# Modulation weights loaded two tiles at a time in a two-block transformer kernel on one Trainium2 core

## What is computed

```python
def _layer(x, ...):                       # first block, two layers
    proj = _rms_norm(x, g_pre) @ w_in     # 2048 -> 5952 columns
    ...                                   # three kinds of attention, gated
    y = concat([o_a, o_b, o_c]) @ w_out   # 2048 -> 2048
    return x + _rms_norm(y, g_post)

def hybrid_layer(x, c, ..., w_mod, b_mod, ...):   # second block, two layers
    mod = silu(c) @ w_mod + b_mod                 # (1, 2048) @ (2048, 6144)
    shift, scale, gate = split(mod, 3)
    h = rms_norm(x, g_pre) * (1.0 + scale) + shift
    ...                                           # window attention, spatial gating, linear attention
    out = y @ w_out
    return x + gate * rms_norm(out, g_post)
```

## Time and profile before

| what | value |
|---|---|
| runs | 3788.1, 3803.92 and 3804.02 us, median 3803.92 |
| profiled execution, own time | 3796.71 us |
| its span, first to last instruction | 3795.0 us |
| mean granted TensorE clock | 0.964 of full |
| PE busy | 3564.3 us, 94% |
| DVE busy | 1820.6 us, 48% |
| ACT busy | 1111.3 us, 29% |
| POOL busy | 221.5 us, 6% |
| DMA | 430.32 MB, mean 113 GB/s |

### The profile page before, as it was taken

The page is one execution under the profiler, slowest core; times in us unless marked ns, Lnnn a source line. Parts: engine busy times, 40 slices in busy tenths (PEclk is TensorE's granted clock), DMA queues, the critical chain, the costliest instruction groups (busy, mean ns, idle before and its releaser), DMA issues.

```text
span 3795.0 us, 51974 instructions
## 1 busy us (share of the span) xinstructions
PE 3564.3 (94%) x17037; PEld 2820.2 (74%) x17037; DVE 1820.6 (48%) x3194; ACT 1111.3 (29%) x1784; POOL 221.5 (6%) x410
## 2 busy tenths in 40 slices
PE   6999999899799999988997999999997999999998
PEld 5777877658677787775786888788786888778786
DVE  4554664434555547643356332635544432625553
ACT  3232242122222322510323222532322322522331
POOL 1101001001211010010010000000000000000000
PEclk9999999989999999998998999999898999999999
DMA  7625415115655353150354333032143333033142
GB/s 231 192 94 185 138 34 168 57 35 190 207 179 185 103 189 92 41 174 12 112 176 151 98 96 98 18 97 78 56 150 108 89 100 99 23 92 100 45 144 99
DMA packets 186920, 430.32 MB, mean 113 GB/s; under 512 B 21238, under 2 KB 28849, under 8 KB 180312
## 3 DMA queue, kind: packets, MB, share of 16 engines
q1 hardware_dynamic: 151720, 302.30, 24.6%
q0 software_dynamic: 32064, 104.44, 9.4%
q10 hardware_dynamic: 2928, 21.02, 1.3%
HBM read 406.61 MB, written 24.75 MB: 114 GB/s over the span
## 4 chain that ended last, share of the span: by engine, by line
PE 77%; DMA 10%; DVE 7%; issue 5%; ACT 1%; DVEq 0%; POOLq 0%; SPq 0%; ACTq 0%; POOL 0%
PE bank L635 19%; PE bank L637 19%; PE bank L636 19%; DMA wmod<-in_w_mod 9%; PE bank L676 4%; PE bank L694 3%; PE bank L668 2%; PE bank L685 2%; DVE macc L1327 2%; PE bank L827 1%; PE bank L655 1%; PE bank L805 1%; PE bank L816 1%; PE bank L664 1%; PE bank L881 1%
## 5 line engine op out<-in xcount | busy, mean ns | idle before, releaser
L635 PE MATMUL bank<-wlo,act_hi 128*128 128x512 f32 (+1 forms) x3968 | 1558.1, 393 | 49.8 <-DVE zone L1356 28.5
L637 PE MATMUL bank<-whi,act_lo 128*128 128x512 f32 (+1 forms) x3968 | 1541.0, 388 | 0.0
L636 PE MATMUL bank<-whi,act_hi 128*128 128x512 f32 (+1 forms) x3968 | 1541.0, 388 | 0.0
L1014 ACT ACTIVATE whi<-stage 128x1024 fp32r<-128x1024 f32 (+1 forms) x496 | 515.1, 1048 | 1512.6 <-PE bank L637 644.8
L635 PEld LDWEIGHTS bank<-wlo,act_hi 128*128 128x128 f32 x3968 | 749.5, 189 | 228.9 <-DVE zone L1356 33.1
L1312 DVE TENSOR_TENSOR wlo<-stage,whi 128x1024 fp32r<-128x1024 f32 (+1 forms) x496 | 597.0, 1208 | 624.4 <-ACT whi L1014 620.6
L637 PEld LDWEIGHTS bank<-whi,act_lo 128*128 128x128 f32 x3968 | 749.1, 189 | 153.4
L636 PEld LDWEIGHTS bank<-whi,act_hi 128*128 128x128 f32 x3968 | 749.9, 189 | 146.5
L1327 DVE SCALAR_TENSOR_TENSOR macc<-wmod,csil,macc 128x512 f32<-128x512 f32 x360 | 270.4, 751 | 440.0 <-DMA wmod<-in_w_mod 432.7
L2053 POOL DMA_DIRECT2D wmod<-in_w_mod x384 | 206.2, 537 | 1793.7 <-DVE macc L1322 1054.5
L1120 ACT ACTIVATE zone<-bank 128x512 f32<-128x512 f32 x128 | 76.4, 597 | 149.2 <-PE bank L685 149.0
(11 more groups left out here) (211 smaller groups left out, 2508.0 us busy)
## 6 DMA issues: line engine op xcount, KB each, us to landing
stage<-in_w_in SPq DMA_DIRECT2D x352, 512.0 KB, 3.7
wmod<-in_w_mod POOLq DMA_DIRECT2D x384, 256.0 KB, 3.2
stage<-in_w_out SPq DMA_DIRECT2D x128, 512.0 KB, 3.9
out<-Y ACTq DMA_DIRECT2D x20, 1024.0 KB, 5.1
zone<-out SPq DMA_DIRECT2D x4, 4096.0 KB, 14.5
stage<-in_w_in SPq DMA_DIRECT2D x16, 320.0 KB, 4.2
Y<-in_x SPq DMA_DIRECT2D x4, 1024.0 KB, 9.2
rpb_tiles<-rpb_pad POOLq DMA_DIRECT2D x16, 224.0 KB, 7.2
```

The source lines that it names most:

```text
L635: pe.matmul(out, hi_x, lo_w, start=(k == 0), stop=False)
L636: pe.matmul(out, hi_x, hi_w, start=False, stop=False)
L637: mm = pe.matmul(out, lo_x, hi_w, start=False, stop=(k == KC - 1))
L1014: act.activation(whi[:, j % RH, :, 0:width], stage[:, j % RS, :, 0:width], ACT.Copy)\
```

## The change

`wmod` becomes two places of two tiles each, 8 KB in a partition. `mprod` and `junk` lose memory of their own and lie over the second pair, so the total and all addresses behind them stay. A load takes two tiles (512 KB) in one DMA and waits until the pair before the last is used; the credit is 4. VectorE waits once for each pair. In the first block ScalarE writes the squares to `zone` at column `ZK`; in the second, to `mprod` and `junk` as before. What is loaded, summed and multiplied, and in which order VectorE does it, stays.

```diff
-        wmod = sb("wmod", [P, 2, PW])
-        mprod = sb("mprod", [P, PW])
-        junk = sb("junk", [P, PW])
+        wmod = sb("wmod", [P, 2, 2, PW])
...
+        mprod = sb("mprod", [P, PW], at=wmod_at + 8 * PW)
+        junk = sb("junk", [P, PW], at=wmod_at + 12 * PW)
...
-        mod_landed = [count(f"mod_landed{s}", 16 * NIN * KC // 2, 0) for s in range(2)]
-        mod_used = count("mod_used", NIN * KC, 0, credit=2)
+        mod_landed = [count(f"mod_landed{s}", 16 * NIN * KC // 4, 0) for s in range(2)]
+        mod_used = count("mod_used", NIN * KC, 0, credit=4)
...
-                    act.activation((mprod, junk)[t % 2][:, :], LIN[t][:, :], ACT.Square,
+                    squares = (mprod, junk)[t % 2][:, :] if blk else view(ZK + t % 2 * PW, PW)
+                    act.activation(squares, LIN[t][:, :], ACT.Square,
...
             def mod_pair(l, q, i):
+                dve.wait_ge(mod_landed[i % 2].sem, mod_landed[i % 2].at(0, l, 16 * (q * (KC // 4) + i // 2 + 1)))
                 for k in (2 * i, 2 * i + 1):
                     m = q * KC + k
-                    dve.wait_ge(mod_landed[k % 2].sem, mod_landed[k % 2].at(0, l, 16 * (q * (KC // 2) + i + 1)))
                     if k == 0:
                         dve.wait_ge(mod_sum.sem, mod_sum.at(0, l, q))
                         apart(dve)
-                        dve.tensor_scalar(macc[:, :], wmod[:, 0, :], csil[:, 0:1], None, ALU.mult)\
+                        dve.tensor_scalar(macc[:, :], wmod[:, 0, 0, :], csil[:, 0:1], None, ALU.mult)\
...
-                        dve.scalar_tensor_tensor(out=macc[:, :], in0=wmod[:, k % 2, :], scalar=csil[:, k:k + 1],
+                        dve.scalar_tensor_tensor(out=macc[:, :], in0=wmod[:, i % 2, k % 2, :], scalar=csil[:, k:k + 1],
...
             def mod_loads(l, p):
-                for k in range(KC):
-                    pool.wait_ge(mod_used.sem, mod_used.at(0, l, p * KC + k + 1 - 2))
+                for i in range(KC // 2):
+                    pool.wait_ge(mod_used.sem, mod_used.at(0, l, p * KC + 2 * i + 2 - 4))
                     apart(pool)
-                    src = io["w_mod_2"][bass.ds(l, 1), k * P:(k + 1) * P, bass.ds(p * PW, PW)]
-                    pool.dma_start(wmod[:, k % 2, :], src.rearrange("o p n -> (o p) n"))\
-                        .then_inc(mod_landed[k % 2].sem, 16)
+                    src = io["w_mod_2"][bass.ds(l, 1), 2 * i * P:(2 * i + 2) * P, bass.ds(p * PW, PW)]
+                    pool.dma_start(wmod[:, i % 2, :, :], src.rearrange("o (a p) n -> p (o a) n", p=P))\
+                        .then_inc(mod_landed[i % 2].sem, 16)
```

More of the change, by code:

```diff
@@ L200, in build @@
         cgw = sb("cgw", [P, KC, G_RANK], at=wmod_at + 2432)
-        cgw_hl = sb("cgw_hl", [P, KC, 2, G_RANK], F32R, at=sb_at["mprod"])
-        la = sb("la", [P, TT, 256], at=sb_at["junk"])
-        assert sb_at["macc"] == sb_at["junk"] + 4 * PW
+        cgw_hl = sb("cgw_hl", [P, KC, 2, G_RANK], F32R, at=wmod_at + 8 * PW)
+        la = sb("la", [P, TT, 256], at=wmod_at + 12 * PW)
+        assert sb_at["macc"] == wmod_at + 16 * PW
         PP, ZQ, ZT, ZK, ZV = 0, 4096, 8192, 10240, 12288
```

## The result

The changed kernel takes 3748.67 us (median of four runs, 3748.2 to 3749.45) against 3801.41 us for the kernel before: a ratio of 0.9869, 95% interval 0.9846 to 0.9892, or 52.7 us less. The forecast was 3743 us, in a range of 3726 to 3784. The profiled execution's own time is 3749.45 us, its span 3747.8.

The account below looks back on a forecast made before the run. TensorE was taken as the bound, with late modulation tiles lengthening its panels. From the profiled execution's 3796.7 us, 57.3 came off and 0 was added for the start, 3739.4; half the distance to the median made 3743 us, range 3726 to 3784.

Parts of the forecast that it names:

- What bounds and what a wait costs: TensorE bounds; VectorE's 432.7 us wait for tiles counts only where TensorE stalls, through bank copies at panel ends.
- Distance, not number: Modulation loads: a reload issued a whole pair earlier hides its landing; fewer, larger loads are not what helps.
- L: Modulation loads: time from the end of a pair's use to the landing of its reload.
- budget of 9.4: Wide panels: us between a place's uses, two TensorE steps less one pair of accumulations; 4 us to spare.
- The sum: Panels 2, 10 and 11 return 49.4 us, six more panels 6.3, eleven others 1.6: 57.3 us in total.
- budget of 5.5 us: Narrow panels: two steps of 3.52 us less 1.5; a pair may come slightly late, costed at nothing.
- the bound of 5 us: Narrow panels: if the ring's cover is gone, 0.3 us in each of 16 steps.
- The start: Start of the kernel: the first two loads carry 1 MB rather than 512 KB; cost 0, at most 2.6 us.
- one common line: Start of the kernel: were all DMA traffic served in one line, the extra 0.52 MB would cost 1.3 to 2.6 us.
- A: Panels 10, 11 and 2: staged weights hold VectorE, about half of 49.4 us stays; 3772 us, chance 0.14.
- B: All 192 steps with modulation tiles: a pair's reload becomes the bound, 96 us lost; 3839 us, chance 0.04.
- C: Modulation loads: only one pair in flight, or the row sum's wait holds VectorE; no change, 3800 us, chance 0.06.

Follow-up runs that it names:

- the kernel before with copies first: Kernel before, loads unchanged; in eight panels with modulation tiles VectorE copies its two banks before the last pair of tiles: 3772.18 us, ratio 0.9942.
- the four places: Changed kernel with four places of one tile, one tile a load (384 loads of 256 KB): 3737.92 us, ratio 0.9851; run again, 3731.88 us.
- the single place: Changed kernel with 512 KB pair loads but one place and credit 2, each load waiting for the pair just used: 4107.39 us, ratio 1.081.
- the narrow panel's copies first: Changed kernel; in panel 10 alone VectorE copies its two banks before the last pair of tiles: 3736.72 us, ratio 0.9837; run again, 3733.91 us.
- squares alone: Kernel before with only the first block's squares written to `zone`: 3800.21 us over ten runs, ratio 0.9997.
- the run without reloads: Changed kernel with only the first four modulation tiles loaded and used over and over: 3739.84 us, ratio 0.9855.
- the runs with four and eight DMAs: Changed kernel with each pair loaded by four DMAs of 128 columns, 3763.89 us (0.9912), or eight of 64, 3895.87 us (1.0261).

## Why the prediction was right

**What bounds and what a wait costs.** Right. The 362 us of waiting that VectorE lost (432.7 less 71.1) brought 53 us, and they came where the price was read, in the length of panels. The reading that VectorE's bank copies behind a late pair carry it is shown by the kernel before with copies first, half the gain with the waits left in.

**Distance, not number.** Right, by the four places and the single place. The landing of a pair was taken as 4 to 5 us from the row for 512 KB on SP's queue; it is 4.5. L is 5.3 us against a budget of 9.4, so 4 us are to spare, as forecast. The Trainium skill (DMA: Bandwidth & Descriptors, section "Anatomy of one DMA — SWDGE (gpsimd) path") has 2.0 us plus the bytes at 436 GB/s, from which an estimate of 3.2 us follows; the measured landing is 1.3 us longer.

**The sum.** Panel 2 gave 12.4 of 12.5 us forecast, panel 10 18.2 of 18.7, panel 11 13.3 of 18.2. The whole was forecast as 57.3 us and is 55.7, read at the start of the second block. The three panels make 43.9 of it; the other panels and the starts of attention make 11.8, where 7.9 were in the sum. Of the surplus 1.5 us is TensorE's wait for Y at the start of attention, now 11.3 us and before 12.8, which the forecast had named and left out. The sum also left out three panels: it took eleven at 0.15 us, and beside panels 2 and 10 and the six of the earlier trace rows fourteen more take tiles, which would have made it 0.4 us larger. That the total is only 1.6 us off is partly luck: panel 11 was put 4.9 us too high and the other panels 3.9 too low.

**The step that was off.** "There a pair may come late by part of a microsecond. I cost that at nothing, since the ring of split weights lets VectorE run up to three steps ahead." The budget of 5.5 us was right and L is 5.3 to 5.8, so pairs are late by 0.4 us a turn; and the ring does cover the splits, for panel 10 itself is at 29.4. What it doesn't cover are the bank copies at the panel's end, which have no buffer ahead of them and stand behind the last pair. They cost 2 x 2.4 = 4.8 us. That this lies just under the bound of 5 us is luck: the bound was worked out for splits 0.3 us late in each of 16 steps, and the loss came by another way, as the narrow panel's copies first show.

**Smaller sizes.** VectorE's wait for tiles was to be below 40 us and is 71.1, all of the excess without effect but for panel 11. An issue takes POOL 0.711 us instead of 0.536, where up to twice as much had been allowed for. The start: the staged tile that matters lands 0.3 us later than in the earlier trace rows:

```profile
6.43 26.45 DMA stage<-in_w_in
```

The forecast was 0 with 2.6 as the bound. In two more profiles with the old loads (squares alone, and the kernel before with copies first) that tile landed at 32.75 and 33.29 us, before at 32.60 and after at 32.88, so the 0.3 lies inside the spread, and the larger load on POOL's queue doesn't hold up SP's by the 1.3 to 2.6 us of one common line. The rule cited from the Trainium skill (same page, section "Queues, rings and completion order"), turns between the queues that have work, agrees with this. It isn't free for every form: with the same bytes cut into 16 loads (eight DMAs a pair) the tile landed at 34.79, 1.9 us later than after the change. Squares: 0 forecast, none seen (ratio 0.9997).

**The predicted time.** It added half the distance from the profiled execution to the median, 3.6 us, and came out at 3743. The median is 3748.7. Of the 5.7 us between, 1.6 are the gain (55.7 instead of 57.3). The other 4.1 are the second block, 8.5 us longer in the profiled execution, less the 3.6 that were added and the 0.8 by which the median lies under that execution. Most of the 8.5 us is one stretch of linear attention (130.8 us before, 138.8 after), whose length is not set by the change, and no sum over panels can forecast it.

**The rivals.** A falls by the run without reloads. B's mechanism is real and its threshold lies where the runs with four and eight DMAs leave it, between 7.4 and 10.3 us, but the reload takes 5.3. C: two pairs are indeed in flight, as the single place shows by contrast.

## What to carry to other kernels

Count buffers in units of use: two places for tiles that are consumed two at a time are one buffer, and each load has only the rest of one step to land. Compare the time from the end of a use to the landing with the distance to the next use, for the shortest step too, and look at what stands behind the wait on the same engine: a copy that frees a bank or a place should not stand behind a wait for data that nobody needs yet. The total of an engine's waits is no price; the lengths of equal stretches, with and without the work in question, are.

## What was not expected of the hardware

POOL's issue time followed the number of rows of a DMA and not its bytes. A load of one tile (128 rows) is 0.536 us; one of two tiles (256 rows) is 0.71 us, whether a row is 2 KB, 512 or 256 bytes. Splitting a load on this queue therefore costs a full issue for each part, one after the other: eight in 5.64 us.

How long the clock stays low in one and the same stretch is not the same from one execution to the next. The first layer's linear attention took 139.9 us in one profiled execution of the changed kernel (clock 0.87) and 129.7 in another (0.96), the same instructions in the same order. Two such stretches move a kernel by more than 15 us with nothing changed, so a difference of that size is to be read from the windows of the stretches that the edit touches. What decides it, no run here shows.
